# Attention jobs of a repeated layer that turn normed probabilities and give feature-major values, with three gate units dealt between them

## What is computed

```python
def sliding_window_attention(q, k, v, sinks):      # 16 heads of 64, 2 key/value heads
    ...
    s = jnp.where(mask, q @ k * scale, -jnp.inf)   # blocks of 128 queries, 256 keys
    m = jnp.maximum(jnp.max(s, axis=-1, keepdims=True), sink)
    p = jnp.exp(s - m)
    p = p / (jnp.sum(p, axis=-1, keepdims=True) + jnp.exp(sink - m))
    o = p @ v

def second_block(x, ...):
    for l in range(2):
        h = rmsnorm_2(x, norm_mix[l])
        q, k, v, u, ug, ga, gb = jnp.split(h @ w_in[l], SPLITS, axis=-1)
        a_out = sliding_window_attention(rope(norm(q)), rope(norm(k)), v, sinks[l])
        c_out = silu(layernorm(depthwise_conv_31(u * jax.nn.sigmoid(ug)))) @ w_conv_out[l]
        merged = jax.nn.sigmoid(ga) * a_out + jax.nn.sigmoid(gb) * c_out
        x = x + merged @ w_out[l]
        x = x + (jax.nn.silu(g) * up) @ w_down[l]      # g, up = rmsnorm_2(x) @ w_gate_up[l]
```

## Time and profile before

| | us |
|---|---|
| median of 3 runs (2561.84 to 2570.46) | 2567.66 |
| the profiled execution | 2573.36 |
| its span, first to last instruction | 2571.5 |
| PE busy | 2448.3 (95%) |
| DVE, ACT, POOL busy | 1287.1, 879.8, 182.9 |

### The profile page before, as it was taken

The page is one execution under the profiler, slowest core; times in us unless marked ns, Lnnn a source line. Parts: engine busy times, 40 slices in busy tenths (PEclk is TensorE's granted clock), DMA queues, the critical chain, the costliest instruction groups (busy, mean ns, idle before and its releaser), DMA issues.

```text
span 2571.5 us, 30241 instructions
## 1 busy us (share of the span) xinstructions
PE 2448.3 (95%) x11256; PEld 1960.3 (76%) x11256; DVE 1287.1 (50%) x1896; ACT 879.8 (34%) x1405; POOL 182.9 (7%) x137
## 2 busy tenths in 40 slices
PE   7999998979999979999989999999999898999999
PEld 6876787768888857876667888888877677788887
DVE  6456445344443246767344444333877434544433
ACT  4534443343332233323432333223233343433222
POOL 3000021020000020010011000001010001100001
PEclk9999799989999989999589999999999779999999
DMA  5310023112222213210001222323211001222221
GB/s 200 115 50 18 33 94 117 53 66 82 98 98 99 98 49 125 82 66 34 17 34 66 98 96 91 106 99 109 98 67 51 32 1 66 82 98 98 96 100 65
DMA packets 29200, 202.24 MB, mean 79 GB/s; under 512 B 3232, under 2 KB 3872, under 8 KB 5408
## 3 DMA queue, kind: packets, MB, share of 16 engines
q1 hardware_dynamic: 27072, 195.05, 21.4%
q10 hardware_dynamic: 2016, 5.71, 0.6%
HBM read 198.64 MB, written 2.10 MB: 78 GB/s over the span
## 4 chain that ended last, share of the span: by engine, by line
PE 87%; DVE 5%; ACT 4%; issue 4%; DMA 0%; ACTq 0%; POOL 0%; DVEq 0%; POOLq 0%
PE bank L335 23%; PE bank L337 22%; PE bank L336 22%; PE bank L1663 3%; PE bank L1687 2%; PE bank L757 2%; ACT w_hi L256 2%; PE bank L784 1%; PE bank L1676 1%; PE bank L285 1%; PE bank L1664 1%; DVE h L1389 1%; PE bank L773 1%; PE bank L1710 1%; PE bank L1711 1%
## 5 line engine op out<-in xcount | busy, mean ns | idle before, releaser
L335 PE MATMUL bank<-x_hi,w_hi 128*128 128x512 f32 x2080 | 834.8, 401 | 53.3 <-DVE x_lo L326 30.2
L337 PE MATMUL bank<-x_hi,w_lo 128*128 128x512 f32 x2080 | 818.2, 393 | 0.0
L336 PE MATMUL bank<-x_lo,w_hi 128*128 128x512 f32 x2080 | 817.8, 393 | 0.0
L260 DVE TENSOR_TENSOR w_lo<-w_raw,w_hi 128x2048 fp32r<-128x2048 f32 x180 | 414.9, 2306 | 415.7 <-ACT w_hi L256 415.7
L335 PEld LDWEIGHTS bank<-x_hi,w_hi 128*128 128x128 f32 x2080 | 396.1, 190 | 143.8 <-DVE x_lo L326 32.5
L256 ACT ACTIVATE w_hi<-w_raw 128x2048 fp32r<-128x2048 f32 x180 | 344.1, 1914 | 397.5 <-PE bank L337 395.7
L337 PEld LDWEIGHTS bank<-x_hi,w_lo 128*128 128x128 f32 x2080 | 395.2, 190 | 84.7
L336 PEld LDWEIGHTS bank<-x_lo,w_hi 128*128 128x128 f32 x2080 | 396.3, 191 | 81.8 <-issue 2.9
L337 PE MATMUL bank<-f_hi,w_lo 128*128 128x512 f32 x528 | 208.6, 395 | 0.0
L336 PE MATMUL bank<-f_lo,w_hi 128*128 128x512 f32 x528 | 208.6, 395 | 0.0
L335 PE MATMUL bank<-f_hi,w_hi 128*128 128x512 f32 x528 | 208.6, 395 | 0.0
(11 more groups left out here) (308 smaller groups left out, 2525.5 us busy)
## 6 DMA issues: line engine op xcount, KB each, us to landing
w_raw<-w_d SPq DMA_DIRECT2D x184, 1024.0 KB, 4.8
h<-x_d ACTq DMA_DIRECT2D x4, 512.0 KB, 7.7
out_d<-h SPq DMA_DIRECT2D x4, 512.0 KB, 4.9
tab<-rope_d ACTq DMA_DIRECT2D x2, 640.0 KB, 4.1
memT<-mem_d ACTq DMA_DIRECT2D x1, 1024.0 KB, 5.3
stage<-cmask_d ACTq DMA_DIRECT2D x1, 384.0 KB, 8.7
pos_i<-pos_d ACTq DMA_DIRECT2D x1, 256.0 KB, 8.6
gains<-pack_d ACTq DMA_DIRECT2D x1, 228.5 KB, 5.9
```

The source lines that it names most:

```text
L260: dve.tensor_tensor(w_lo[:, u.slot, :], w_raw[:, u.slot, :], w_hi[:, u.slot, :], ALU.subtract).then_inc(lo_ready, 1)
L335: pe.matmul(dst, wh[:, k, cols], hi[:, kx_, 0:width], start=start, stop=False)
L336: pe.matmul(dst, wh[:, k, cols], lo[:, kx_, 0:width], start=False, stop=False)
L337: return pe.matmul(dst, wl[:, k, cols], hi[:, kx_, 0:width], start=False, stop=stop)
```

## The change

Five things, all in the second block's pass (twice per launch):

1. **Jobs.** ACT divides the exponentials by their sum before they are turned (`scaled`, in place, two instructions a job); `lprob` has three buffers instead of two. `values` swaps its operands: V is the weight (64 columns), the turned probabilities move (128 columns), and the two heads go to the two halves of the partitions, so the result is feature-major. `back` and DVE's `lo_s` are gone. The lags are 2 and 3 steps for turn and values. `scores` issues the two heads' products, then the two masks.
2. **Gates.** Units 14, 15 and 16 are dealt as 48 chunks between jobs: 3 ahead of step 0, 2 or 3 in most steps up to 21 (`gate_chunks`). The tile order of the rope work is changed: k first, and the last q tile's `head_rows(8)` and `rotate(8)` come after unit 13. Each sigmoid is `tanh` of half the argument; the factors 0.5 and the added 1 go into instructions that exist.
3. **Layer norm.** Squares are added up by three POOL instructions, so the column sums need 4 products instead of 16; the mean goes to `acc`; the convolution's normed tiles go to `x_hi[4..7]`. The sum is at step 10, the column sums at 15, root 16, rows 18, silu 20, projection 23 to 30.
4. **Splits** of units 17 to 21 are in halves (`L_SPLIT_AT`).
5. **Output projection.** `merged_hi` and `merged_lo` start at steps 29 and 30, and the products of its first unit start at step 32; the last chunk (k = 7) is asked for after 24+18+21 other products.

```diff
-        UNIT_TAPS = {2: 7, 3: 7, 4: 10, 5: 10, 6: 10, 7: 10, 8: 11, 9: 11, 10: 4, 11: 4, 12: 4, 13: 4, 14: 8, 15: 1}
-        JOB_TAPS = [2, 2, 3, 2, 3, 3, 3, 3, 2]
+        UNIT_TAPS = {2: 7, 3: 7, 4: 10, 5: 10, 6: 10, 7: 10, 8: 10, 9: 9, 10: 5, 11: 5, 12: 5, 13: 5}
+        JOB_TAPS = [3, 3, 3, 3, 3, 3, 3, 3, 3, 4]
+        V_FILL = 14
+        LAG_T, LAG_V = 2, 3
+        FILL_FIRST, FILL_BANK = 3, (5, 7, 5, 7, 7, 7)
+        FILL_AT = {0: 3, 1: 3, 2: 3, 3: 3, 4: 3, 5: 3, 6: 3, 7: 3, 8: 3, 9: 2, 11: 2, 12: 2, 13: 2, 14: 2, 16: 3, 20: 3, 21: 2}
+        AT_SUM, AT_MEAN, AT_SS, AT_STD, AT_INV, AT_ROWS, AT_SILU, AT_HI, AT_CO = 10, 11, 15, 16, 17, 18, 20, 21, 23
+        L_SPLIT_AT = {5: (17, 0), 6: (17, 1), 10: (18, 0), 11: (18, 1), 22: (19, 0), 23: (19, 1), 27: (20, 0), 28: (20, 1),
+                      31: (21, 0), 32: (21, 1)}
...
+                for e in range(2):
+                    mm = pe.matmul(bank[:, score_bank(j) + e, c0:2 * P], ident_b[:, :], mask_b[:, c0:2 * P], start=False, stop=True)
...
-                        mm = pe.matmul(bank[:, 6, e * HD:(e + 1) * HD], lprobT[:, j % 2, 2 * e + c, :],
-                                       lv[:, i - 1 + c, g * HD:(g + 1) * HD], start=(c == first), stop=(c == 1))
+                for c in range(first, 2):
+                    for e in range(2):
+                        mm = pe.matmul(bank[HD * e:HD * e + HD, 6, 0:P], lv[:, i - 1 + c, g * HD:(g + 1) * HD],
+                                       lprobT[:, j % 2, 2 * e + c, :], start=(c == first), stop=(c == 1))
...
+            head_rows(8)
+            gate_chunks(FILL_FIRST)
             for t in range(STEPS):
                 if t < LJ:
                     scores(t)
+                if t == 1:
+                    rotate(8)
+                if 0 <= t - LAG_T < LJ:
+                    turn(t - LAG_T)
+                gate_chunks(FILL_AT.get(t, 0))
...
+                if 0 <= t - LAG_V < LJ:
+                    values(t - LAG_V)
...
+            out_products(0, (0, 1), (4, 5, 6))
+            pe.wait_ge(lo_ready, Unit(base + V_OUT + 1, L).n + 1)
+            out_products(1, (0,), range(7))
+            out_products(0, (0, 1), (7,)).then_inc(unit_done, 1)
...
+            def scaled(j):
+                c0 = P if block_of(j) == 0 else 0
+                act.wait_ge(A["rec"], L * LJ + j + 1)
+                act.wait_ge(A["exp"], (L * LJ + j) * 3 + 2)
+                for e in range(2):
+                    act.activation(lprob[:, j % 3, e, c0:2 * P], lprob[:, j % 3, e, c0:2 * P], ACT.Copy,
+                                   scale=asm(j, 12, e)).then_inc(A["scaled"], 1)
...
             for t in range(STEPS):
                 if t < LJ:
                     exps(t)
+                if 0 <= t - 1 < LJ:
+                    scaled(t - 1)
+                if 0 <= t - LAG_T < LJ:
+                    copy_turned(t - LAG_T)
```

More of the change, by code:

```diff
@@ L1550, in build @@
         co_done, co_ready, mg_sum, mg_hi, mg_lo = (sem("l_" + n) for n in ("co_done", "co_ready", "mg_sum", "mg_hi", "mg_lo"))
-        A = {n: sem("a_" + n) for n in ("scores", "max", "neg", "sinkd", "exp", "den", "rec", "turned", "turned_copied",
-                                        "pv", "out", "back", "gated")}
+        A = {n: sem("a_" + n) for n in ("scores", "max", "neg", "sinkd", "exp", "den", "rec", "scaled", "turned", "turned_copied",
+                                        "pv", "gated")}
@@ L1633, in layer_pe @@
                 if n in ROPE_UNITS:
-                    for t in pairs(n - ROPE_UNITS[0]):
-                        head_rows(t)
+                    for r in pairs(n - ROPE_UNITS[0]):
+                        head_rows(r)
                 linear_tile(pe, u, 1).then_inc(unit_done, 1)
@@ L1682, in values @@
                 pe.wait_ge(A["turned_copied"], L * LJ + j + 1)
-                if j:
-                    pe.wait_ge(A["out"], L * LJ + j)
-                for e in range(2):
-                    for c in range(first, 2):
-                        mm = pe.matmul(bank[:, 6, e * HD:(e + 1) * HD], lprobT[:, j % 2, 2 * e + c, :],
-                                       lv[:, i - 1 + c, g * HD:(g + 1) * HD], start=(c == first), stop=(c == 1))
-                mm.then_inc(A["pv"], 1)
-            def back(j):
-                pe.wait_ge(A["out"], L * LJ + j + 1)
-                if j:
-                    pe.wait_ge(A["gated"], L * LJ + j)
-                pe.transpose(bank[:, 7, 0:P], lo_s[:, j % 2, :], ident[:, :]).then_inc(A["back"], 1)
@@ L1774, in layer_act @@
             take_rows(act, norm)
-            for n in range(V_CO - 1):
+            for n in range(V_FILL):
                 u = Unit(base + n, L)
@@ L1843, in copy_turned, with merged_hi @@
                    .then_inc(A["turned_copied"], 1)
+            def merged_hi(k):
+                if k == 4:
+                    act.wait_ge(unit_done, L * V_N + base + V_CO + 2)
+                act.wait_ge(mg_sum, L * 8 + k + 1)
+                act.activation(x_hi[:, k, :], sgb[:, k, :], ACT.Copy, scale=0.5).then_inc(mg_hi, 1)
             for t in range(STEPS):
```

375 lines of the change are left out of this document (193 added, 182 removed).

## The result

The changed kernel takes 2526.46 us (median of 4 runs, 2522.82 to 2529.42) against 2569.06 us of the kernel before on the same chip; the ratio is 0.9834, 95% interval 0.9803 to 0.9865. That is 42.6 us less, where 89.4 were forecast, and 6 us outside the range. The profiled execution has a span of 2521.0 us.

The account below looks back on a forecast made before the run. PE was taken to set the end everywhere, above all through its low clock. Per pass 65.5 us removed less 20.8 added is 44.7, for both 89.4, so 2478 us from 2567.66; range 2445 to 2520 (own range 2460 to 2500).

Parts of the forecast that it names:

- Clock: Second block's jobs and tail: gate products among jobs keep TensorE's clock up, 36.1 us a pass removed.
- start gap: Before the jobs, behind unit 13: PE idles 6.4 us for DVE's add, plus 2.0 us at low clock, a pass.
- Waits removed, back, column sums: Second pass: 16.0 us of PE idle time, 6.7 of back transposes and 2.5 of column sums go.
- Scores and values: PE's job products: fewer form changes save 4.2 us a pass in scores; values at 0.90 us a job add 1.9.
- Rival 1: Scores and values: neighbouring heads run side by side in separate array halves, 40 us in all, 2438 us; chance 0.15.
- Changes of tiling mode: Values: by the skill's rule, 64-column weights bring in the two changes a step that scores lose; about 2487 us.
- Steps 0 to 9: First job steps: PE, with 45.7 us of work against DVE's 42, sets the pace; 1.5 us for collisions.
- ACT in steps 16 to 23: Steps with root and silu table loads: ACT's work delays turn(20) and turn(21), 6.5 us a pass added.
- the ring: In the jobs PE waits for ACT, ACT for DVE, DVE for PE; named after measuring, no size in the forecast.
- Rival 2: Values: dear at 1.68 us a job, 38 us more in all, 2517 us; chance 0.10.
- Rival 3: Steps 15 to 22: ACT's chain sets the pace and its gaps drop the clock, 12 us a pass, 2502; chance 0.08.
- Rival 5: Jobs: no change, since waits and low clock return in new places through longer, deeper chains; 2567 us; chance 0.03.

Follow-up runs that it names:

- run 7: Changed kernel with PE's values moved ahead of turn and chunks, values and gating at lag four, and DVE's half splits a step behind ACT's: 2468.11 us.
- run 10: Changed kernel with PE's values ahead of turn and chunks (lag three kept) and DVE's half splits a step behind ACT's: 2473.73 us.
- run 12: run 7 with tanh in place of the convolution's silu, so no silu table loads and output not the layer's: 2455.97 us.
- run 5: Changed kernel with seven gate chunks instead of three, put ahead of the ninth tile's transposes, one fewer in steps 5 to 8: 2527.73 us.
- run 8: run 7 with the start gap filled by seven gate chunks ahead of the ninth tile's transposes: 2464.95 us.
- run 13: run 7 with DVE's five taps behind unit 13 cut to 16 of 512 columns, part of the convolution left out: 2461.74 us.
- run 14: run 8 with DVE's five taps behind unit 13 cut to 16 of 512 columns: 2455.09 us.

## Why the prediction was wrong

The sign, most of the clock and the length of the start gap were right; the size was not, since one step failed: that PE sets the pace of the jobs.

- *Clock.* Right in the main: the 68 us at 0.52 became a stretch at full clock but for dips. The sum had 2.0 us a pass for what stays low. Measured are six stretches at 0.50, at 1924, 1965, 1999, 2043, 2088 and 2095, in sum:

```profile
sum 37.40, PE 29.05 PEld 21.19 DVE 20.28 ACT 11.54 POOL 5.15; mean PE 4.84 PEld 3.53 DVE 3.38 ACT 1.92 POOL 0.86
```

  By the ratio of the sum (0.454 of the time at the low clock goes at the full one) that is 13.2 us a pass.
- *Waits removed, back, column sums.* The four old waits at whole splits are gone as such, and the column sums take 2011.21-2010.23 = 0.98 us against 0.9 in the sum. No run tests these terms apart.
- *Scores and values.* Too dear on paper. Rival 1's mechanism is true for both: scores and masks of a job went from 1.59 to 0.86 us, 0.73 less against the 0.13 of the sum (4.2 us for 32), and values from 0.84 to 0.59, not up to 0.90. Ahead of the values comes a change of form that the old kernel did not have there, 0.09 us. A step without gate products shows the total: step 17 takes 2017.24-2015.26 = 1.98 us against 3.07. Over 24 full jobs that is 17.5+6.0-2.2 us of PE work where the sum had 4.2-1.9: 19.0 us less PE work. The lower clock took back 13.2-2.0 = 11.2 of it; of the 7.8 left the windows show 6.5, and 1.3 stay unexplained.
- *Changes of tiling mode.* The rule of the Trainium skill (TensorEngine Tiling (Array Packing), Tiling Modes, Key Properties) that was weighed at the values term, that such a change drains TensorE, agrees with these rows: a product that brings another form of weights starts some 0.09 us later than one that doesn't (0.32 against 0.23 behind a gate product, 0.21 against 0.12 behind a mask). The sum's estimate was 0.13. A full step had four such changes and has three: two go with the scores and one comes with the values, since the change behind the values stood behind `back` before. That different tiles work in parallel, which the same section of the Trainium skill also states, agrees with the 0.01 us between the starts of two scores and of two values.
- *Steps 0 to 9: "PE still sets the pace; for collisions 1.5."* This is the step that failed. I compared sums of work, 45.7 us on PE and 42 on DVE, and left out in what order each engine waits for the others. Steps 0 to 9 were to take 45.7+1.5 = 47.2 us. They take 49.43 although PE's work came cheaper, with PE idle for 8.5 of them; in run 7, with the same work, 42.46 and 3.7. The same reasoning gave steps 10 to 15 no idle time at all (7.6 measured) and the last steps 2.5 (9.5 measured, of it 4.8 in three waits for `merged_lo`, which are 1.1 in run 7). Two orders cost 46 to 53 us of the launch (run 10): DVE's half split in the step of ACT's (23 to 27 alone), and PE's values behind the turn and the chunks, with the gating ahead of DVE's taps (23 alone).
- *ACT in steps 16 to 23, 6.5 a pass.* PE is idle for 13.6 us there. The waits forecast at `turn(20)` and `turn(21)` came (2.72 and 2.89 us), and behind the second one of 3.30 for DVE's `x_lo` at the projection's first product. The rest is the ring again: in run 7 the same steps have 37.98-31.39 = 6.6 us idle, which is what the sum had. Removing the silu's tables there gives 4.8 to 6.1 a pass (run 12).
- *Start gap, 6.4.* Its length was right (5.85 us), its price was not: DVE works through it and sets the first maximum (runs 5, 8, 13, 14). Filling it won nothing: without the gap the same time would have been waited a little later.
- *The rivals.* None had the right place. Rival 2 came nearest in time (2517) with dear values, which were cheap. Rival 3 was true in part: steps 16 to 23 lost 7.1 us more than the sum had and some 2 to the clock, of the 12 that it priced, but as much again was lost in each of the other stretches. Rival 5 had the mechanism ("waits come back in new places, as each job's chain is one ACT step longer and one lag deeper"), at a price for all of the gain and a chance of 0.03. Run 10, with the two orders mended, takes 2473.73 us, 4 us from the forecast. That is luck: the cheap scores and values cancel the clock and what is left of the waits.

## What to carry to other kernels

Where engines pass results round in a ring, comparing each one's sum of work does not find the pace. Write out for each engine's step what it waits for and what is queued behind that wait, and count every wait for a result that another engine makes late in its own step of the same number: each such pair (DVE's half split behind ACT's, the gating behind PE's values) cost 11 to 14 us a pass here, and was mended by one step of delay or by moving one call. Each of these prices is this kernel's. A gap of an engine is worth filling only if the next thing that is late waits for that engine.

## What the runs showed of the hardware

Two products with 64 rows each, in separate halves of the array, started 0.01 us apart and ran side by side when they were neighbours in the program (0.86 us a job with masks), and not when a product with 128 rows stood between them (1.59). Eight products with 64-column weights and 128 moving columns started in pairs, 0.01 to 0.02 us apart, and took 0.59 us, whatever the order of the two heads. A product whose weights had another form than the ones before started some 0.09 us later than one of the same form. A table load took 1.28 us; two of them cost ACT 2.85 us, since the activations beside them didn't overlap.

TensorE's granted clock fell from 1.00 to 0.50, its lower level of 1.2 GHz, behind waits of PE, but how long it stayed there did not follow their length: 3.4 us at each of the single waits of 3.79 and 3.80 us, 6.8 us at waits of 2.89 and 3.30 us close together, 3.4 and 13.7 us at waits of 3.53 and 2.83 us. It stayed at 1.00 from 2011 to 2039, over waits of 2.74 and 2.72 us. So the length of the last gap alone, by which I had judged, doesn't tell what the clock does.
